# The one-hot rows of a gate matrix: two scalars in one VectorE instruction, the other rows on POOL

## The chip, the cores and the metric

The kernel runs on one NeuronCore of a Trainium2 chip. Its engines work side by side and meet only at semaphores: TensorE (PE) multiplies matrices into PSUM, VectorE (DVE) and ScalarE (ACT) work on PSUM and SBUF, GpSimd (POOL) on SBUF, and SyncE (SP) issues DMAs. The metric is the device time of one execution in microseconds (us); lower is better.

## The reference, cut to what matters

Four layers run one after another on 256 tokens of width 1024: two of a first kind and two of a second kind. The change lies in the last part of each second-kind layer, a feed-forward with 16384 small experts. A token picks 8 x 16 experts, and each expert number is a pair of key numbers below 128:

```python
cand_i = top_i[:, :, 0, :, None] * N_KEYS + top_i[:, :, 1, None, :]
best_s, best_pos = lax.top_k(cand_s..., PEER_TOPK)
experts = take_along_axis(cand_i..., best_pos)
gate = jax.nn.softmax(best_s, axis=-1)
act = jax.nn.gelu(einsum('td,thkd->thk', t, expert_down[experts]))
return einsum('thk,thkd->td', (gate * act), expert_up[experts])
```

## The kernel before, in words

`peer(l)` doesn't gather experts. It computes all 16384 activations densely, multiplies them by a gate matrix that is zero for experts not picked, and multiplies the product with all of `expert_up`. Everything is fp32, and a weight tile is split into a rounded part `hi` and a rest `lo`, so that three matmul passes give the product.

The weights come in units of 128x1024: 16 of the query projection (`PQ`), 128 of `expert_down`, 128 of `expert_up`. Each unit goes through a ring of three buffers (`RING`): SP loads it into `raw` (L1774), ACT writes `hi` (`head`, L1891), the rest `lo` is written by POOL for the first `BY_POOL` = 86 units (L1795) and by DVE for later ones (`rest`, L2057), then PE uses it: `down(n)` issues 24 matmuls (L1810), `up(x)` 12 (L1843). SP loads a buffer again once `lo` of the unit before in it is written.

Between units 72 (`PQ + FIRST`) and 83 lies **the gate stage**. The three picks of each token (first key number, second key number, softmax gate) have been turned by PE so that a token is a column of `i1T`, `i2T` and `gT`, with its 128 picks along the partitions. For each of 64 groups (`GROUPS`) of 4 tokens (`GROUP`):

- DVE (`one_hots`, L2043) compares `iota` with 4 columns of `i1T` at once into `hot1`, and with 4 columns of `i2T` into `hot2`, two instructions of 512 elements per partition. There are three buffers of each (`HOTS`); from the fourth group on it waits until PE has used the third last.
- ACT (`gated`, L1922) multiplies the four rows of `hot1` by the token's gate, four instructions of 128 elements in place, and signals `gated`.
- PE (`gates`, L1830) multiplies `hot2` with `hot1` for each token, a 128x128 gate matrix each, into one of four PSUM banks. The trace shows 8 matmul records for a group.
- DVE (`into_a`, L2051) multiplies the first 56 columns of the bank into the activations `A`, two groups behind `one_hots`; ACT (`to_a`, L1928) copies the other 72 columns to `A`.

After 11 of the 64 groups (`STAGED`, by `staged_after`: after group 5, 11, 17, 23, 29 and so on to 63) PE does one `down` unit; ACT then takes its result (L1905) and does `head` for the unit three ahead, after which POOL writes that unit's `lo`. ACT's order in the loop is: `gated(g + 1)`, `to_a(g)`, and where a unit was due after group g - 1, its result and a `head`. When the stage is over DVE multiplies the 11 staged units in one instruction (L2097), and PE does the other 61 `down` units. The stage occurs once in each of the two second-kind layers.

## Time and profile before

| | us |
|---|---|
| time, median of 3 executions | 3636.59 (3634.34 to 3645.01) |
| the profiled execution's own time | 3646.36 |
| its span, first to last instruction | 3643.6 |
| PE busy in it | 3080.6 (85%) |
| DVE busy | 2466.6 (68%) |
| ACT busy | 1530.2 (42%) |
| POOL busy | 1040.1 (29%) |

Durations of the profile belong to an execution of 3646.36 us, 2.8 us of them outside the span. The two layers with a gate stage fill the second half of the span: their gate stages lie at about 1856 to 2015 and 2950 to 3111 us from its start. An instruction's duration in the trace overlaps a little with the next one's on DVE, ACT and PE, so how much an instruction of a row adds is read from one start to the next; both are called here by name, duration and pitch. A wait for another engine's semaphore stands as idle time before an instruction; a wait for an SBUF port stands inside its duration.

### The profile page before, as it was taken

The numbers are of one execution on the slowest core, as the hardware profiler recorded it, in microseconds if no ns is written. First come the engines' busy times: TensorE is split into PE (matmuls) and PEld (weight loads), VectorE is DVE, ScalarE is ACT, GpSimd is POOL, SyncE is SP. The second block draws the span as 40 slices with busy tenths as digits, with TensorE's granted clock in tenths as the row PEclk, the third lists the DMA queues.
The fourth block names the chain that finished last, engine by engine and source line by source line (L and its number), as shares of the span: only waits on it lengthen the run. The fifth ranks groups of instructions, "written<-read, shape, count | busy, mean of one in ns | idle before, by whom it ended". The sixth has DMA issues, their size and how long they took to land. (4 is left out here: it accounts for less than half of the span.)

```text
span 3643.6 us, 48268 instructions
## 1 busy us (share of the span) xinstructions
PE 3080.6 (85%) x18164; PEld 2737.8 (75%) x18164; DVE 2466.6 (68%) x3633; ACT 1530.2 (42%) x2506; POOL 1040.1 (29%) x559
## 2 busy tenths in 40 slices
PE   6765899867758997859987999998869987999998
PEld 5654677666646765749977998886759986998887
DVE  5998756569987664537958655665547958655665
ACT  2221443222215432324467444553324467444554
POOL 3355520543555114008941000000007941000000
PEclk9887899988879999769988999999779998999999
DMA  5444444454434444505631566665505631566665
GB/s 211 147 146 145 179 160 152 155 214 150 159 134 185 153 145 179 179 22 183 186 104 36 170 190 185 205 193 156 198 12 181 186 110 41 158 190 186 204 195 162
DMA packets 128230, 568.86 MB, mean 156 GB/s; under 512 B 14155, under 2 KB 24172, under 8 KB 96364
## 3 DMA queue, kind: packets, MB, share of 16 engines
q1 hardware_dynamic: 117916, 505.43, 42.7%
q0 software_dynamic: 9216, 56.63, 4.3%
q8 instruction: 148, 2.42, 0.3%
q10 hardware_dynamic: 864, 3.67, 0.2%
q14 instruction: 86, 0.70, 0.1%
HBM read 551.52 MB, written 15.20 MB: 156 GB/s over the span
## 5 line engine op out<-in xcount | busy, mean ns | idle before, releaser
L1810 PE MATMUL e_ps<-k_hhi,e_hi 128*128 128x256 f32 x2304 | 651.6, 283 | 30.2 <-POOL e_lo L1795 30.2
L1810 PE MATMUL e_ps<-k_hlo,e_hi 128*128 128x256 f32 x2304 | 645.9, 280 | 0.0
L1810 PE MATMUL e_ps<-k_hhi,e_lo 128*128 128x256 f32 x2304 | 644.3, 280 | 0.0
L2057 DVE TENSOR_TENSOR e_lo<-e_raw,e_hi 128x1024 fp32r<-128x1024 f32 x372 | 455.9, 1226 | 193.9 <-ACT e_hi L1891 193.9
L1891 ACT ACTIVATE e_hi<-e_raw 128x1024 fp32r<-128x1024 f32 x544 | 571.0, 1050 | 26.7 <-DMA e_raw<-down 26.1
L1795 POOL TENSOR_TENSOR e_lo<-e_raw,e_hi 128x1024 fp32r<-128x1024 f32 x172 | 444.6, 2599 | 344.1 <-ACT e_hi L1891 343.5
L721 DVE TENSOR_TENSOR f_wlo<-f_raw,f_whi 128x2048 fp32r<-128x2048 f32 x156 | 390.5, 2519 | 191.8 <-ACT f_whi L539 191.8
L539 ACT ACTIVATE f_whi<-f_raw 128x2048 fp32r<-128x2048 f32 x156 | 296.2, 1911 | 505.7 <-DMA f_raw<-ws 391.1
L1810 PEld LDWEIGHTS e_ps<-k_hhi,e_hi 128*128 128x128 f32 x2304 | 436.3, 189 | 31.6 <-POOL e_lo L1795 31.2
L1810 PEld LDWEIGHTS e_ps<-k_hlo,e_hi 128*128 128x128 f32 x2304 | 436.5, 189 | 0.0
L1810 PEld LDWEIGHTS e_ps<-k_hhi,e_lo 128*128 128x128 f32 x2304 | 435.9, 189 | 0.0
L1843 PE MATMUL e_ps<-e_hi,e_ghi 128*128 128x512 f32 x1024 | 315.4, 389 | 1.2 <-DVE e_glo L2066 1.2
L1843 PE MATMUL e_ps<-e_hi,e_glo 128*128 128x512 f32 x1024 | 315.3, 389 | 0.0
L1843 PE MATMUL e_ps<-e_lo,e_ghi 128*128 128x512 f32 x1024 | 315.2, 389 | 0.0
L412 PE MATMUL f_psA<-f_whi,k_hhi 128*128 128x512 f32 x672 | 276.9, 412 | 44.0 <-DVE f_wlo L721 38.4
L774 DVE SCALAR_TENSOR_TENSOR f_cy<-f_vpad,f_par,f_cy 128x256 f32<-128x256 f32 x480 | 313.9, 725 | 0.0
L389 PE MATMUL f_psA<-k_hhi,f_whi 128*128 128x256 f32 x640 | 200.0, 312 | 117.2 <-DVE f_wlo L721 103.8
L690 POOL TENSOR_TENSOR f_x<-f_x,k_cact 128x2048 f32<-128x2048 f32 x48 | 216.6, 4513 | 273.4 <-DMA f_x<-ada 273.4
L692 POOL TENSOR_TENSOR f_x<-f_x 128x1024 f32<-128x1024 f32 x144 | 268.7, 1866 | 11.3
L412 PE MATMUL f_psA<-f_wlo,k_hhi 128*128 128x512 f32 x672 | 271.9, 405 | 0.0
L412 PE MATMUL f_psA<-f_whi,k_hlo 128*128 128x512 f32 x672 | 271.2, 404 | 0.0
L1940 ACT ACTIVATE e_ghi<-e_a 128x256 fp32r<-128x256 f32 x256 | 107.0, 418 | 344.8 <-PE e_ps L1843 344.8
(335 smaller groups left out, 5749.1 us busy)
## 6 DMA issues: line engine op xcount, KB each, us to landing
f_raw<-ws SPq DMA_DIRECT2D x156, 1024.0 KB, 5.0
e_raw<-down SPq DMA_DIRECT2D x288, 512.0 KB, 3.7
e_raw<-up SPq DMA_DIRECT2D x256, 512.0 KB, 3.7
f_x<-ada POOLq DMA_DIRECT2D x48, 1024.0 KB, 5.3
s_raw<-ws SPq DMA_DIRECT2D x24, 1024.0 KB, 5.1
mod_parts<-f_x POOLq DMA_DIRECT2D x48, 128.0 KB, 2.0
s_parts<-mod_parts SPq DMA_DIRECT2D x8, 768.0 KB, 8.7
f_x<-out SPq DMA_DIRECT2D x4, 1024.0 KB, 5.1
```

The costliest lines, as they stand in the source:

```text
L389: last = nc.tensor.matmul(psA[:, n % 4, f * T:(f + 1) * T], w[:, c:c + P], x[:, kt, :], start=kt == 0 and i == 0, stop=kt == KT - 1 and i ...
L412: last = nc.tensor.matmul(psA[:, (n + t) % 4, :], x[:, kt, ts_], w[:, k * CH:(k + 1) * CH], start=v == 0 and k == 0 and i == 0, stop=v == ...
L539: nc.scalar.activation(w_hi[:, u % NW, :], raw[:, u % NRAW, :], ACT.Copy).then_inc(S["hi_ready"], 1)
L690: own.link(nc.gpsimd.tensor_tensor(a3, a3, by_c, ALU.mult))
L692: own.link(nc.gpsimd.tensor_tensor(ada[:, 0:half], ada[:, 0:half], ada[:, half:2 * half], ALU.add))
L721: V.tensor_tensor(w_lo[:, u % NW, :], raw[:, u % NRAW, :], w_hi[:, u % NW, :].bitcast(F32), ALU.subtract).then_inc(S["lo_ready"], 1)
L774: ins = V.scalar_tensor_tensor(cy[:, ft, :], v, w, cy[:, ft, :], ALU.mult, ALU.add)
L1795: nc.gpsimd.tensor_tensor(lo[:, i % RING, :], raw[:, i % RING, :], hi[:, i % RING, :].bitcast(F32), ALU.subtract).then_inc(S["lo_pool"], 1)
L1810: last = nc.tensor.matmul(psD(n), w, h, start=kt == 0 and i == 0, stop=kt == KT - 1 and i == 2)
L1843: last = nc.tensor.matmul(psY(t, c), g[:, b, tok], w[:, r, c * CH:(c + 1) * CH], start=x == 0 and i == 0, stop=x == NE - 1 and i == 2)
L1891: nc.scalar.activation(hi[:, i % RING, :], raw[:, i % RING, :], ACT.Copy).then_inc(S["hi_ready"], 1)
L2057: V.tensor_tensor(lo[:, i % RING, :], raw[:, i % RING, :], hi[:, i % RING, :].bitcast(F32), ALU.subtract).then_inc(S["lo_dve"], 1)
```

## The change

`hot1` is now written by DVE row by row with the gate in it: one `tensor_scalar` of 128 elements for a token, with two per-partition scalars, `(iota == i1T[:, t]) * gT[:, t]`, four for a group. `hot2` is written by POOL, one `tensor_scalar` of 128 elements for a token with one per-partition scalar, `iota == i2T[:, t]`. ACT's `gated` and its semaphore are gone: PE waits for `hot1_ready` and `hot2_ready`. POOL stops writing `lo` at unit 75 (`BY_POOL` = 75), then does its 256 rows; units 75 to 85 get their `lo` from DVE, ten inside the loop of groups, four groups behind the unit that they follow, and one behind the loop.

```diff
-BY_POOL = PQ + FIRST + STAGED + RING
+BY_POOL = PQ + FIRST + RING
...
+                pool.wait_ge(S["in_const"], 32)
+                pool.wait_ge(S["picks_copied"], 2)
+                for g in range(GROUPS):
+                    if g >= HOTS:
+                        pool.wait_ge(S["w_mm"], g - HOTS + 1)
+                    for k in range(GROUP):
+                        t = g * GROUP + k
+                        ins = nc.gpsimd.tensor_scalar(hot2[:, g % HOTS, k, :], iota[:, :], i2T[:, t:t + 1], None, ALU.is_equal)
+                    ins.then_inc(S["hot2_ready"], 1)
...
-                    pe.wait_ge(S["gated"], g + 1)
+                    pe.wait_ge(S["hot1_ready"], g + 1)
                     pe.wait_ge(S["hot2_ready"], g + 1)
...
-                def gated(g):
-
-                    act.wait_ge(S["hot1_ready"], g + 1)
-                    for k in range(GROUP):
-                        row = hot1[:, g % HOTS, k, :]
-                        ins = nc.scalar.activation(row, row, ACT.Copy, scale=gT[:, g * GROUP + k:g * GROUP + k + 1])
-                    ins.then_inc(S["gated"], 1)
...
-                gated(0)
                 for g in range(GROUPS):
-                    if g + 1 < GROUPS:
-                        gated(g + 1)
                     to_a(g)
...
-                    tokens = slice(g * GROUP, (g + 1) * GROUP)
-                    for hot, picks, ready in ((hot1, i1T, "hot1_ready"), (hot2, i2T, "hot2_ready")):
-                        V.tensor_tensor(hot[:, g % HOTS, :, :], iota[:, :].rearrange("p (a n) -> p a n", a=1).to_broadcast([P, GROUP, NE]),
-                                        picks[:, tokens].rearrange("p (a n) -> p a n", n=1).to_broadcast([P, GROUP, NE]),
-                                        ALU.is_equal).then_inc(S[ready], 1)
+                    for k in range(GROUP):
+                        t = g * GROUP + k
+                        ins = V.tensor_scalar(hot1[:, g % HOTS, k, :], iota[:, :], i1T[:, t:t + 1], gT[:, t:t + 1], ALU.is_equal, ALU.mult)
+                    ins.then_inc(S["hot1_ready"], 1)
...
                 for g in range(GROUPS):
-                    one_hots(g)
+                    gated(g)
                     if g >= 2:
                         into_a(g - 2)
+                    n = staged_after(g - 4) if g >= 4 else None
+                    if n is not None:
+                        rest(n + RING)
                 into_a(GROUPS - 2)
                 into_a(GROUPS - 1)
+                for g in range(GROUPS - 4, GROUPS):
+                    n = staged_after(g)
+                    if n is not None:
+                        rest(n + RING)
```

DVE's row in the gate stage before, from the group whose `into_a` is the seventh (the `e_hot` names are `hot1` and `hot2`):

```order
L2051 TENSOR_TENSOR e_a<-e_ps,e_a 128x56x4
L2043 TENSOR_TENSOR e_hot_6867<-e_iota,e_i1T 128x512
L2043 TENSOR_TENSOR e_hot_6868<-e_iota,e_i2T 128x512
L2051 TENSOR_TENSOR e_a<-e_ps,e_a 128x56x4
L2043 TENSOR_TENSOR e_hot_6867<-e_iota,e_i1T 128x512
L2043 TENSOR_TENSOR e_hot_6868<-e_iota,e_i2T 128x512
```

And DVE's row there in the change:

```order
L2049 TENSOR_TENSOR e_a<-e_ps,e_a 128x56x4
L2042 TENSOR_SCALAR e_hot_6867<-e_iota,e_i1T,e_gT 128x128 x4
L2049 TENSOR_TENSOR e_a<-e_ps,e_a 128x56x4
L2055 TENSOR_TENSOR e_lo<-e_raw,e_hi 128x1024
L2042 TENSOR_SCALAR e_hot_6867<-e_iota,e_i1T,e_gT 128x128 x4
L2049 TENSOR_TENSOR e_a<-e_ps,e_a 128x56x4
```

Two wide compares became four short instructions, and the rest of a weight unit stands between two groups. ACT's row around the first staged unit before:

```order
L1922 ACTIVATE e_hot_6867<-e_hot_6867,e_gT 128x128 x4
L1928 ACTIVATE e_a<-e_ps 128x72x4
L1905 ACTIVATE e_b<-e_ps 128x256
L1891 ACTIVATE e_hi<-e_raw 128x1024
L1922 ACTIVATE e_hot_6867<-e_hot_6867,e_gT 128x128 x4
L1928 ACTIVATE e_a<-e_ps 128x72x4
```

And in the change:

```order
L1930 ACTIVATE e_a<-e_ps 128x72x4 x7
L1915 ACTIVATE e_b<-e_ps 128x256
L1901 ACTIVATE e_hi<-e_raw 128x1024
L1930 ACTIVATE e_a<-e_ps 128x72x4 x6
L1915 ACTIVATE e_b<-e_ps 128x256
L1901 ACTIVATE e_hi<-e_raw 128x1024
```

The gate copies that stood behind each `head` are gone from ACT. POOL's whole row for `peer` in the change against before:

```order
 L996 ISA
 L1791 UNCONDITIONAL_BRANCH
-L1795 TENSOR_TENSOR e_lo<-e_raw,e_hi 128x1024 x86
+L1795 TENSOR_TENSOR e_lo<-e_raw,e_hi 128x1024 x75
+L1805 TENSOR_SCALAR e_hot_6868<-e_iota,e_i2T 128x128 x256
 L1761 UNCONDITIONAL_BRANCH
```

Eleven long instructions left POOL, and 256 short ones came behind the other 75.

## Rows read from the trace of the kernel before

**Rows 1.** Stretches: length, each engine's busy time, granted TensorE clock, DMA share, GB/s.

```profile
1856.00:2015.00 159.00, 118.11 (x810) 111.10 (x809) 127.05 (x196) 114.00 (x345) 31.38 (x13) 0.87 0.15 44
...
2950.00:3111.00 161.00, 119.41 (x830) 112.14 (x829) 124.24 (x195) 114.76 (x347) 34.64 (x14) 0.88 0.16 48
```

**Rows 2.** Groups of 1860 to 2012: busy us, mean ns; idle before, its releasers.

```profile
L1830 PE MATMUL e_ps<-e_hot,e_hot 128*128 128x128 f32 x512 | 84.7, 328 | 40.9 <-ACT e_hot L1922 36.5 <-DVE e_hot L2043 4.3
...
L2043 DVE TENSOR_TENSOR e_hot<-e_iota,e_i2T 128x512 f32<-128x512 f32 x64 | 67.5, 1055 | 0.0
L2043 DVE TENSOR_TENSOR e_hot<-e_iota,e_i1T 128x512 f32<-128x512 f32 x63 | 42.9, 681 | 0.0
L2051 DVE TENSOR_TENSOR e_a<-e_ps,e_a 128x224 f32<-128x224 f32 x64 | 24.8, 388 | 29.0 <-PE e_ps L1830 27.5
...
L1922 ACT ACTIVATE e_hot<-e_hot,e_gT 128x128 f32<-128x128 f32 x252 | 79.8, 392 | 2.1 <-DVE e_hot L2043 2.1
...
L1891 ACT ACTIVATE e_hi<-e_raw 128x1024 fp32r<-128x1024 f32 x11 | 11.6, 1058 | 0.0
...
L1795 POOL TENSOR_TENSOR e_lo<-e_raw,e_hi 128x1024 fp32r<-128x1024 f32 x10 | 25.7, 2573 | 119.5 <-ACT e_hi L1891 119.5
```

**Rows 3.** Timeline behind one staged unit: start us, length us, engine, line.

```profile
1943.18 1.95 PE L1830 MATMUL e_ps<-e_hot,e_hot 128*128 128x128 f32 x16
1947.54 1.26 PE L1830 MATMUL e_ps<-e_hot,e_hot 128*128 128x128 f32 x8 [2.41 <-ACT e_hot L1922]
...
1945.78 0.38 DVE L2051 TENSOR_TENSOR e_a<-e_ps,e_a 128x224 f32<-128x224 f32 x1
1946.09 0.68 DVE L2043 TENSOR_TENSOR e_hot<-e_iota,e_i1T 128x512 f32<-128x512 f32 x1
1946.68 2.84 DVE L2043 TENSOR_TENSOR e_hot<-e_iota,e_i2T 128x512 f32<-128x512 f32 x1
...
1946.22 1.27 ACT L1922 ACTIVATE e_hot<-e_hot,e_gT 128x128 f32<-128x128 f32 x4
...
1946.41 2.58 POOL L1795 TENSOR_TENSOR e_lo<-e_raw,e_hi 128x1024 fp32r<-128x1024 f32 x1 [9.74 <-ACT e_hi L1891]
```

**Rows 4.** The stretch that follows it, columns as in rows 1.

```profile
1949.40:1954.80 5.40, 4.99 (x23) 4.70 (x23) 4.42 (x10) 3.92 (x13) 0.00 (x0) 0.50 0.33 99
```

**Rows 5.** Timeline: the first gate matmul, and the instruction behind the stage.

```profile
1860.50 0.77 PE L1830 MATMUL e_ps<-e_hot,e_hot 128*128 128x128 f32 x2 [4.34 <-DVE e_hot L2043]
...
2012.04 3.09 DVE L2097 TENSOR_TENSOR e_a<-e_a,e_b 128x2816 f32<-128x2816 f32 x1 [2.90 <-ACT e_b L1905]
```

**Rows 6.** DVE's tensor_scalar, two lines (ns min/median/max) and a timeline row.

```profile
L1655 DVE TENSOR_SCALAR s_ys<-s_ys,s_stat x4: 346/348/348, 1587.2 to 2685.5; 128x256 f32<-128x256 f32 x4
L1655 DVE TENSOR_SCALAR s_ya<-s_ya,s_stat x4: 479/480/482, 1587.7 to 2686.1; 128x512 f32<-128x512 f32 x4
...
369.75 2.67 DVE L896 TENSOR_SCALAR f_cy<-f_cy,f_par 128x256 f32<-128x256 f32 x8
```

**Rows 7.** POOL's nearest instructions, grouped or by line, in ns.

```profile
L1449 POOL TENSOR_SCALAR s_stat<-s_stat 128x8 f32<-128x8 f32 x6 | 1.2, 200 | 134.5 <-DVE s_stat L1539 91.8 <-DVE s_stat L1591 42.5
L1453 POOL MEMSET s_ones<- 128x128 f32 x2 | 0.4, 202 | 0.0
...
L692 POOL TENSOR_TENSOR f_x<-f_x x144: 724/1335/4539, 44.4 to 1434.1; 128x1024 f32<-128x1024 f32 x48, 128x512 f32<-128x512 f32 x48, 128x256 f32<-128x256 f32 x48
```

**Rows 8.** Timeline of DVE and POOL instructions that overlap, in two places.

```profile
70.17 1.36 POOL L692 TENSOR_TENSOR f_x<-f_x 128x512 f32<-128x512 f32 x1
71.61 0.81 POOL L692 TENSOR_TENSOR f_x<-f_x 128x256 f32<-128x256 f32 x1
71.74 0.95 DVE L774 SCALAR_TENSOR_TENSOR f_cy<-f_vpad,f_par,f_cy 128x256 f32<-128x256 f32 x1
...
1704.72 2.41 POOL L1795 TENSOR_TENSOR e_lo<-e_raw,e_hi 128x1024 fp32r<-128x1024 f32 x1 [0.18 <-ACT e_hi L1891]
1706.44 0.72 DVE L2025 TENSOR_SCALAR e_bx<-e_bp 128x32 uint32<-128x32 uint32 x1
```

More of the change, by code:

```diff
@@ L1744, in peer @@
         names = """in_const in_keys raw0 raw1 raw2 in_x out_x hi_ready lo_pool lo_dve unit_done psd_read score_mm sc_copied
-            dve_step t_sub t_exp iv_ready picks_mm picks_copied hot1_ready hot2_ready gated w_mm w_read_dve w_read_act
+            dve_step t_sub t_exp iv_ready picks_mm picks_copied hot1_ready hot2_ready w_mm w_read_dve w_read_act
             staged_mult weighted g_hi_ready g_lo_ready gate_mm gate_ready prod_done x_done""".split()
@@ L2035, in key_numbers, with gated @@
                     own.step(V.tensor_reduce(iv[:, 0:2, :, h * 16:(h + 1) * 16].rearrange("p k t s -> p (k t) s"), hots[:, :, :, :], AX.X, ALU.add))
-                def one_hots(g):
+                def gated(g):
                     if g >= HOTS:
                         dve.wait_ge(S["w_mm"], g - HOTS + 1)
-                    tokens = slice(g * GROUP, (g + 1) * GROUP)
-                    for hot, picks, ready in ((hot1, i1T, "hot1_ready"), (hot2, i2T, "hot2_ready")):
-                        V.tensor_tensor(hot[:, g % HOTS, :, :], iota[:, :].rearrange("p (a n) -> p a n", a=1).to_broadcast([P, GROUP, NE]),
-                                        picks[:, tokens].rearrange("p (a n) -> p a n", n=1).to_broadcast([P, GROUP, NE]),
-                                        ALU.is_equal).then_inc(S[ready], 1)
+                    for k in range(GROUP):
+                        t = g * GROUP + k
+                        ins = V.tensor_scalar(hot1[:, g % HOTS, k, :], iota[:, :], i1T[:, t:t + 1], gT[:, t:t + 1], ALU.is_equal, ALU.mult)
+                    ins.then_inc(S["hot1_ready"], 1)
                 def into_a(g):
```

## The prediction, made before the change was run

> **What bounds the kernel now.** I read the stretches first. Over the gate stages PE is busy for only 118 of 159 us and 119 of 161 us, at a mean granted clock of 0.87 and 0.88 of full [rows 1]. DVE (127 us) and ACT (114 us) are busier than they look necessary for 64 groups, and POOL has 31 us. So these two stretches, 320 us of 3644, are where an exchange between DVE, ACT and POOL can move the end.
>
> Next I read the groups of one stage by shape. Each of the 64 groups costs DVE two compares of 512 elements and one `into_a`. Their pitches stand in the timeline: `into_a` starts at 1945.78, the next compare at 1946.09, the next at 1946.68 [rows 3], so 0.31 and 0.60 us. A group is 2 x 0.60 + 0.31 = 1.51 us, 64 of them 97 us. The second compare has a mean of 1055 ns where the first has 681 [rows 2]: 64 x 0.374 = 24 us more. The timeline shows what that is: the compare at 1946.68 lasts 2.84 us because POOL's `lo` instruction runs from 1946.41 to 1948.99, and it ends 0.53 us behind it [rows 3]. Eleven such collisions of 2.17 us make the 24. DVE then waits 29 us for PE [rows 2]. 97 + 24 + 29 = 150, and the stage from the first gate matmul to the multiply behind it lasts 2012.04 - 1860.50 = 151.5 us [rows 5]. The account closes.
>
> Why does DVE wait for PE if PE is idle for 41 us? PE's idle time is put down to ACT's gate copies, 36.5 us [rows 2]. Behind each staged unit ACT does a result, a `head` of 1.06 us [rows 2] and only then the copies at 1946.22 for the next group; PE, whose two ready groups ended at 1945.13, stands for 2.41 us [rows 3]. A few microseconds later the granted clock is 0.50, that is 1.2 GHz instead of 2.4, for 5.4 us [rows 4]. There PE is busy and slow. So the stage is bound by a loop DVE, ACT, PE with three faults in each of 11 rounds: the copies behind a `head`, the collision with POOL, and the half clock behind the idle time.
>
> **What the change removes.** ACT loses 256 copies a stage, 80 us of duration [rows 2], and PE no longer waits for ACT's order. DVE loses both compares, 1.20 us a group, and the collisions with the long POOL instruction, 24 us a stage. POOL loses 11 instructions of 2.57 us.
>
> **What it adds on DVE.** A `tensor_scalar` of 256 elements takes 348 ns and one of 512 takes 480 [rows 6], so 128 elements less save 66 ns. With two scalars, eight of 256 elements last 2.67 us [rows 6]; the last one's duration being 0.41 (0.35 and about 0.06 for the second scalar), the pitch is (2.67 - 0.41) / 7 = 0.32 us. For 128 elements I get 0.32 - 0.066 = 0.256 us, four of them 1.02, and with `into_a` 1.33 us a group. Against 1.51 that is little: cut in four, the work of the same 512 elements costs more than one wide compare did, and the gain on DVE is only that `hot2` went elsewhere. The moved `lo` adds 11 x 1.15 us = 12.7 us; its price is not in the gate stage of before, and I take POOL's 2.57 halved less a short overlap, since both engines do the same instruction and the compare of 512 elements on DVE (0.60) scales to 1.14 for 1024 elements. Nothing is past it in DVE's queue but the next group, and POOL and PE have up to three groups of rows in hand. DMA isn't touched: SP's load of a later unit waits for this `lo`, some 2 us later than before, but three units of about 9 us lie between.
>
> **What it adds on POOL.** Nothing in the trace is this instruction: one input of 128 elements, one per-partition scalar. The nearest below is the `tensor_scalar` of 8 elements, 200 ns, and a memset of 128 elements, 202 ns. The nearest above is a two-input instruction: 128x256 takes at least 724 ns [rows 7] and 128x1024 takes 2573 [rows 2], 2.41 ns an element, so 128 elements would take 724 - 308 = 416 ns. One input at half that rate makes 200 + 144 = 344 ns, which I take; the ends are 200 and 416. A gain below nothing is excluded, since it is work that POOL did not have.
>
> **How the two disturb each other.** DVE's `tensor_scalar` in fp32 from SBUF to SBUF collides with POOL: at 1706.44 one of 32 elements lasts 0.72 us, until POOL's instruction ends at 1707.13 [rows 8]. The price of turns can be read from the first layers: POOL's instruction of 512 elements ends at 71.53, its next of 256 ends at 72.42, and the DVE instruction in between ends its own turn 0.27 us behind that [rows 8]. From end to end 0.89 us pass, of which 0.27 are DVE's turn, so POOL's turn is 0.62 where alone it takes 0.724: 0.10 us of its fixed part runs beside DVE's turn. DVE's turn is its streaming time alone. For the change: POOL's turn 0.344 - 0.10 = 0.24 us (bounds 0.10 and 0.32), DVE's turn 0.066 + 0.02 = 0.09. If both always took turns, four pairs last 1.32 us, and a DVE group 1.32 + 0.31 = 1.63; if POOL's turns fall wholly beside `into_a` and DVE's fixed parts, 1.33 remain. I take 1.50, in the middle.
>
> The Trainium skill ("SBUF — State Buffer", Who interferes with whom) says that a VectorE instruction in a two-port mode and a GpSimd instruction exclude each other for the whole instruction, whoever starts first. The row at 1706.44 agrees; the row at 71.61 limits it to less than the duration. What the rule would make of the time by its words is the last rival. The same notes ("VectorE: DVE Perf Modes", The TRN2 errata) advise tiles of at least 512 elements because each instruction pays a fixed cost, which speaks against the cut in four; by the rows 1.02 against 0.60 us it is true here, and the sum above holds it already.
>
> **The sum.** 64 x 1.50 = 96 us; the moved `lo` 12.7; a wait at each staged unit, because PE is away for 2.9 us while DVE may run only three groups ahead, and `lo` waits for a `head`: 11 x 0.7 = 7.7 us (an estimate: three groups of 1.5 us cover the unit, but not the `head` of 1.06 behind it); the first gate matmul comes 0.6 us later, since POOL makes its four rows after its last `lo`; the last unit and its result 3.2 us. Together 120 us. PE needs less: 8 records of about 0.12 us, 0.95 us, for 64 groups and 11 x 2.9, 93 us at full clock. Against 151.5 the stage is 31 us shorter, and both stages 62. Behind the stage DVE does one `lo` more ahead of its multiply, 1.15 us in a stretch where PE has three units ready: nothing is lost. The profiled execution would go from 3646.4 to 3584, and the median from 3636.6 to **3574 us**. With a POOL turn of 0.10 and 1.33 us a group it is 109 us, 85 saved, 3552; with a turn of 0.32 and no overlap (4 x 0.41 + 0.31 = 1.95) it is 149 us, 5 saved, 3632.
>
> **The rivals.**
> - *The turns eat the gain.* POOL's instruction is nearer to the two-input row, pairs cost 0.41 us or a little more, the waits move from ACT to the port: 3625 to 3640, say 3632. For it: a software loop per element on POOL, shown by 2.41 ns an element. Chance 0.12.
> - *POOL becomes the bound, slower than before.* A per-partition scalar and a compare may cost POOL more than any row shows. The stage is worse than before when a group costs over (151.5 - 24) / 64 = 1.99 us, that is when POOL's turn passes 0.41. At a turn of 0.60 a group is 4 x 0.69 = 2.76 us, the stage 201 us, the kernel 99 us slower: 3735. Against it: the 8-element row has fixed costs of only 200 ns. Chance 0.10.
> - *The clock stays low.* If PE runs the gate matmuls at 1.2 GHz throughout, a group takes PE 1.75 us, the stage 64 x 1.75 + 32 = 144 and with the start 147: 9 us saved, 3628. For it: rows 4. Against it: the 2.4 us of idle time ahead of it goes. Chance 0.07.
> - *DVE doesn't get its fast form* with a compare and two scalars: 0.32 us each, but then no turns with POOL. 4 x 0.32 + 0.31 = 1.6, stage 126, 3586. Chance 0.07.
> - *The port is held for whole durations*, as the page says: 0.34 for POOL and 0.34 for DVE, 2.72 us a group, stage 198, two stages 93 us longer, 3730. The row at 71.61 speaks against it. Chance 0.04.
>
> **How the numbers follow.** My forecast, a stage of 109 to 135 us, has 0.60. A measurement of this kernel can tell about 0.3%, 11 us. Faster by more than that: 0.60, the slow DVE form 0.07, part of the first and third rival 0.08, in all 0.75. Within: 0.11. Slower: 0.14. The range from 3545 to 3640 leaves out the two slow rivals and the best corner of the forecast.
>
> **What would show it.** Right: between the first gate matmul and the multiply behind the stage 120 us in place of 151.5; DVE's new instruction at a mean of 0.34 to 0.45 us with POOL's at about 0.35 to 0.45; PE's idle time in the stage below 20 us and put down to DVE or POOL; granted clock above 0.95. Wrong: POOL's instruction above 0.5 us, a POOL without idle time and PE waiting for it; a clock of 0.50 over most of the stage; or DVE waiting for ACT's `head` ahead of the moved `lo` for more than 1 us a time.

## The result and the profile after

The changed kernel takes 3661.53 us, median of 6 executions (3657.72 to 3667.01), where the kernel before took 3639.14 on the same chip, median of 6 (3631.52 to 3645.01). The ratio is 1.0072, with a 95% interval from 1.0052 to 1.0092: slower by 0.7%, 22 us. The prediction said 3574, with a range up to 3640. It had the wrong sign, and the result lies 21.5 us outside the range.

The first and the last row of a gate stage, in the timeline of the changed kernel (start, length, engine, line, in brackets the idle time before), answer to [rows 5]:

```profile
1860.51 0.77 PE L1840 MATMUL e_ps<-e_hot,e_hot 128*128 128x128 f32 x2 [5.87 <-POOL e_hot L1805]
...
2023.38 3.08 DVE L2102 TENSOR_TENSOR e_a<-e_a,e_b 128x2816 f32<-128x2816 f32 x1
```

The stage lasts 2023.38 - 1860.51 = 162.9 us where it was 151.5. The second layer's stage lasts 162.7 where it was 151.1. The two differences, 11.4 and 11.6 us, are 23 us, as much as the medians differ by (22). The two profiled executions differ by less, 18 us in their spans; the other 5 lie outside the gate stages and are not traced here. Every stage length below is read between these two rows, in the first and in the second layer.

The stretch 1875 to 1970 lies inside the stage in every kernel of this study. Here it is, for the kernel before and then for the changed one, in the columns of [rows 1] (length; busy us of PE, PEld, DVE, ACT, POOL; granted clock; DMA share; GB/s):

```profile
1875.00:1970.00 95.00, 72.15 (x475) 67.92 (x474) 78.13 (x122) 70.56 (x216) 18.02 (x7) 0.84 0.13 40
```

```profile
1875.00:1970.00 95.00, 65.48 (x477) 61.42 (x475) 66.41 (x202) 23.47 (x53) 95.00 (x154) 0.93 0.12 39
```

ACT fell from 71 to 23 us, DVE from 78 to 66, and the granted clock rose from 0.84 to 0.93: ACT's gate copies and most of the slow clock are gone. But POOL is busy for 95.00 of 95 us. The groups of one stage (1860 to 2012) show who waits, in the columns of [rows 2]:

```profile
L1840 PE MATMUL e_ps<-e_hot,e_hot 128*128 128x128 f32 x496 | 75.7, 306 | 50.7 <-issue 25.4 <-DVE e_hot L2042 17.6 <-POOL e_hot L1805 7.6
...
L2042 DVE TENSOR_SCALAR e_hot<-e_iota,e_i1T,e_gT 128x128 f32<-128x128 f32 x247 | 75.3, 373 | 0.0
L2049 DVE TENSOR_TENSOR e_a<-e_ps,e_a 128x224 f32<-128x224 f32 x61 | 23.5, 385 | 44.8 <-PE e_ps L1840 44.8
L2055 DVE TENSOR_TENSOR e_lo<-e_raw,e_hi 128x1024 fp32r<-128x1024 f32 x10 | 13.2, 1323 | 2.8 <-ACT e_hi L1901 2.8
...
L1805 POOL TENSOR_SCALAR e_hot<-e_iota,e_i2T 128x128 f32<-128x128 f32 x248 | 152.7, 638 | 0.0
```

PE no longer waits for ACT at all, yet it is idle for 51 us in place of 41, and DVE waits for PE for 45 us in place of 29. The releasers named here don't name the bound: PE and DVE wait for each other (17.6 and 44.8 us), and 25.4 us stand under "issue", with no releaser in the profile. The engine to look for is the one with no idle time, and that is POOL; the runs below test it. The timeline has all its rows of the stage in one line, and the line's own entry has the durations (ns, min/median/max):

```profile
1858.01 157.39 POOL L1805 TENSOR_SCALAR e_hot<-e_iota,e_i2T 128x128 f32<-128x128 f32 x256
```

```profile
L1805 POOL TENSOR_SCALAR e_hot<-e_iota,e_i2T x512: 596/602/1681, 1858.0 to 3122.9; 128x128 f32<-128x128 f32 x171
```

256 instructions of a median 0.602 us follow each other for 157.4 us, 0.615 each. The stage is that queue: it starts when four rows are there and ends 8.0 us behind the last one (1858.01 + 157.39 = 2015.40).

The mean of the rows is 638 ns and their median 602, so a few rows are much longer than the rest. They are the rows that meet one of DVE's moved `lo`. One such pair, DVE's and POOL's:

```profile
1910.64 1.30 DVE L2055 TENSOR_TENSOR e_lo<-e_raw,e_hi 128x1024 fp32r<-128x1024 f32 x1 [0.30 <-ACT e_hi L1901]
```

```profile
1911.08 1.33 POOL L1805 TENSOR_SCALAR e_hot<-e_iota,e_i2T 128x128 f32<-128x128 f32 x1
```

The row takes 1.33 us in place of 0.60: it ends at 1912.41, 0.47 us behind `lo`. The first stage has ten such rows, one for each `lo` between its groups, 7.3 us more than the usual 0.60 in all; the ten of the second stage cost 8.8 us. On a queue without idle time all of this is time of the stage. So the moved `lo` costs twice, once on DVE and once on POOL.

### The profile page after: what moved, and what is told of

It is laid out like the page before. It is cut to its first block and busy times, and to the rows that moved or that the text cites. A ratio compares the mean times of both kernels' runs of the same rounds, so it can differ in the third digit from the quotient of the medians.

```text
span 3661.7 us, 48526 instructions
## 1 busy us (share of the span) xinstructions
PE 3077.7 (84%) x18164; PEld 2735.5 (75%) x18164; DVE 2435.0 (66%) x3911; ACT 1383.6 (38%) x1994; POOL 1290.5 (35%) x1049
## 5 line engine op out<-in xcount | busy, mean ns | idle before, releaser
L2055 DVE TENSOR_TENSOR e_lo<-e_raw,e_hi 128x1024 fp32r<-128x1024 f32 x394 | 484.2, 1229 | 206.2 <-ACT e_hi L1901 205.8
L1795 POOL TENSOR_TENSOR e_lo<-e_raw,e_hi 128x1024 fp32r<-128x1024 f32 x150 | 382.3, 2564 | 91.8 <-ACT e_hi L1901 90.4
L1805 POOL TENSOR_SCALAR e_hot<-e_iota,e_i2T 128x128 f32<-128x128 f32 x512 | 316.0, 640 | 0.0
```

Of the source, the lines that this page charges most:

```text
L1795: nc.gpsimd.tensor_tensor(lo[:, i % RING, :], raw[:, i % RING, :], hi[:, i % RING, :].bitcast(F32), ALU.subtract).then_inc(S["lo_pool"], 1)
L1805: ins = nc.gpsimd.tensor_scalar(hot2[:, g % HOTS, k, :], iota[:, :], i2T[:, t:t + 1], None, ALU.is_equal)
L2055: V.tensor_tensor(lo[:, i % RING, :], raw[:, i % RING, :], hi[:, i % RING, :].bitcast(F32), ALU.subtract).then_inc(S["lo_dve"], 1)
```

## The experiments

### The price of POOL's instruction

`probe_forms` adds a few instructions of each form at the end of POOL's program, when PE is through with the gate matrices, and nothing else (one execution, 3652.18 us):

```diff
+                for i in range(6):
+                    ins = G.tensor_scalar(row(i), iota[:, :], i2T[:, i:i + 1], None, ALU.is_equal)
...
+                    ins = G.tensor_scalar(row(i), iota[:, :], 5.0, None, ALU.is_equal)
...
+                    ins = G.tensor_scalar(row(i), iota[:, :], i2T[:, i:i + 1], None, ALU.mult)
...
+                    ins = G.tensor_scalar(row(i)[:, 0:8], iota[:, 0:8], i2T[:, i:i + 1], None, ALU.is_equal)
...
+                for i in range(3):
+                    ins = G.tensor_scalar(four(i), wide, i2T[:, i:i + 1], None, ALU.is_equal)
...
+                    ins = G.tensor_tensor(row(i), iota[:, :], i2T[:, i:i + 1].to_broadcast([P, NE]), ALU.subtract)
```

> The changed kernel, and behind POOL's 256 rows, where POOL has nothing else to do, seven short series of POOL instructions into a buffer that nobody reads any more: (1) the row instruction of the change, 128 elements, compare with a per-partition scalar; (2) the same with an immediate; (3) multiply in place of compare; (4) 8 elements; (5) 512 elements; (6) a two-input subtract of 128 elements; (7) a two-input subtract of 512. Theory A (the price is POOL's own fixed cost of a per-partition scalar): (1) stays at 0.60 us away from DVE's instructions, (3) and (4) lie within 0.15 us of it, (2) falls to 0.30 to 0.35, (5) costs 0.3 to 0.5 more than (1). Theory B (the price is per element, a slow loop for the compare): (4) is near 0.25, (5) near 1.8 us. Theory C (the 0.60 is mostly waiting for the port behind DVE): (1) falls below 0.45 here. The series add about 20 us of POOL beside the rest of the layer; the time stays within 0.3% of the changed kernel's 3661.

Its lines, each with ns min/median/max (DVE was at work at times, so the minimum is the undisturbed value), and the timeline's row for the first six:

```profile
L1815 POOL TENSOR_SCALAR e_hot<-e_iota,e_i2T x12: 601/602/603, 2004.4 to 3116.4; 128x128 f32<-128x128 f32 x12
L1819 POOL TENSOR_SCALAR e_hot<-e_iota x12: 526/1490/3035, 2008.0 to 3124.5; 128x128 f32<-128x128 f32 x12
L1823 POOL TENSOR_SCALAR e_hot<-e_iota,e_i2T x12: 593/601/1672, 2017.0 to 3131.0; 128x128 f32<-128x128 f32 x12
L1827 POOL TENSOR_SCALAR e_hot<-e_iota,e_i2T x12: 301/310/1257, 2022.6 to 3134.1; 128x8 f32<-128x8 f32 x12
L1831 POOL TENSOR_SCALAR e_hot<-e_iota,e_i2T x6: 1561/1654/2527, 2025.6 to 3137.9; 128x512 f32<-128x512 f32 x6
L1835 POOL TENSOR_TENSOR e_hot<-e_iota,e_i2T x12: 395/489/1382, 2031.2 to 3143.4; 128x128 f32<-128x128 f32 x12
L1839 POOL TENSOR_TENSOR e_hot<-e_iota,e_i2T x6: 1041/1222/2018, 2035.4 to 3147.1; 128x512 f32<-128x512 f32 x6
```

```profile
2004.40 3.49 POOL L1815 TENSOR_SCALAR e_hot<-e_iota,e_i2T 128x128 f32<-128x128 f32 x6 [1.41 <-PE e_ps L1875]
```

And a row of the changed kernel's timeline, eleven of its POOL rows beside DVE's gated rows:

```profile
1899.96 6.48 POOL L1805 TENSOR_SCALAR e_hot<-e_iota,e_i2T 128x128 f32<-128x128 f32 x11
```

From 8 to 128 elements the duration grows by 300 ns, 2.50 ns an element; from 128 to 512 by 960 ns, 2.50 again. So the instruction costs 0.28 us and 2.50 ns an element with **one** input, no less than the two-input `lo` (2.41 ns in the prediction). A multiply costs what the compare costs; the pointer to the scalar (the scalar is read from SBUF, not given in the instruction) adds 601 - 526 = 75 ns; a `tensor_tensor` whose second input is broadcast costs less, (1041 - 395) / 384 = 1.68 ns an element. Alone the pitch is (3.49 - 0.60) / 5 = 0.578 us; beside DVE's gated rows it is (6.48 - 0.60) / 10 = 0.588. The instruction is dear by its elements, and DVE's gated rows have next to no part in its price. The theory of a large fixed cost falls with the 8-element row.

`rows8` asks whether the rest of the prediction's sum holds once POOL's rows are cheap. The buffers are cleared once, and each row has 8 elements, so the kernel leaves out most of the gate matrix:

```diff
-                        ins = nc.gpsimd.tensor_scalar(hot2[:, g % HOTS, k, :], iota[:, :], i2T[:, t:t + 1], None, ALU.is_equal)
+                        ins = nc.gpsimd.tensor_scalar(hot2[:, g % HOTS, k, 0:8], iota[:, 0:8], i2T[:, t:t + 1], None, ALU.is_equal)
```

> The changed kernel with POOL's 256 row instructions cut to 8 of the 128 elements each (the rest of hot2 stays at zero from one memset, so most of the gate matrix is missing); all other instructions, waits and their numbers are the change's. From the forms run a row then costs POOL 0.29 us start to start, near the price that the prediction had assumed. Theory A (the price of the POOL row was the only wrong term of the prediction's sum): the stage falls from 163 to 112 to 126 us, the kernel to 3565 to 3590. Theory D (the rest of the sum was wrong as well: DVE's turns, waits at the staged units, PE's clock): the stage stays above 135 us, 3610 or more.

Measured: 3568.24 against 3627.89, ratio 0.9834 (0.981 to 0.9857), stages of 119.9 and 118.9 us. The stretch 1875 to 1970 and POOL's group in it:

```profile
1875.00:1970.00 95.00, 78.51 (x635) 75.46 (x635) 79.59 (x262) 31.22 (x70) 71.86 (x199) 0.98 0.17 50
```

```profile
L1807 POOL TENSOR_SCALAR e_hot<-e_iota,e_i2T 128x8 f32<-128x8 f32 x199 | 72.1, 412 | 20.6 <-PE e_ps L1842 20.6
```

POOL now waits for PE for 20.6 us and is no longer the bound. The prediction's stage of 120 us and its 62 us saved are there (-60), as soon as POOL's row is not 0.60. DVE's groups of the whole first stage (1855 to 1975) tell how the 120 us come about:

```profile
L2044 DVE TENSOR_SCALAR e_hot<-e_iota,e_i1T,e_gT 128x128 f32<-128x128 f32 x246 | 69.4, 351 | 0.0
L2051 DVE TENSOR_TENSOR e_a<-e_ps,e_a 128x224 f32<-128x224 f32 x64 | 24.8, 389 | 15.6 <-PE e_ps L1842 15.6
L2057 DVE TENSOR_TENSOR e_lo<-e_raw,e_hi 128x1024 fp32r<-128x1024 f32 x11 | 13.5, 1225 | 6.9 <-ACT e_hi L1903 6.9
```

A gated row (one of the four instructions of `hot1`) has a mean of 351 ns, nearly the 346 without POOL (`dve_all`, below), so a group costs DVE about 1.35 us. 64 x 1.35 = 86 us, 12.5 of `lo` and 22.5 of waits (15.6 + 6.9) are the 120, to within 1 us.

`rows64` is the same edit with 64 elements, and leaves out half of the gate matrix. It puts POOL at a price between the two, to find where its queue takes over:

```diff
+                        ins = nc.gpsimd.tensor_scalar(hot2[:, g % HOTS, k, 0:64], iota[:, 0:64], i2T[:, t:t + 1], None, ALU.is_equal)
```

> As the run with 8 elements a row, with 64 (half of hot2's columns stay zero). From the forms run a row costs POOL 0.286 + 56 x 0.00247 = 0.42 us start to start, 1.70 a group. Theory A (POOL's queue binds wherever four rows cost more than DVE's 1.5 to 1.6 us a group): the stage is 64 x 1.70 + 11 x 0.7 + 6 = 123 to 132 us, the ratio to the kernel before 0.985 to 0.990, between 8 elements (0.983, 119 us) and 128 (1.007, 163 us), and nearer to 8. If the turns at the port were what costs, the time would lie halfway, at a stage of about 141 us and a ratio of 0.995.

Measured: 3605.41 against 3639.80, 0.9905 (0.9881 to 0.9929), stages of 132.6 and 133.2 us, both just above what was expected:

```profile
1875.00:1970.00 95.00, 74.68 (x575) 71.11 (x574) 75.05 (x243) 28.16 (x63) 92.09 (x190) 0.95 0.15 45
```

190 rows in 92.1 us are 0.485 each. The probe's 8-element row (0.301), less the 0.024 by which rows overlap (0.602 - 0.578), and 56 x 2.5 ns give 0.42. So some 0.06 us a row is what DVE adds here. By the durations of single rows about half of it is the eight rows of this stretch that start beside a `lo` (each about 1.0 us longer), and the other half comes from gated rows. With 8, 64 and 128 elements the stage lasts 119, 133 and 163 us. The last step is POOL's queue, 256 x (0.615 - 0.485) = 33 us against 30 measured; at 8 elements another bound holds.

### Which half of the change costs, and which pays

`pool_part` keeps only POOL's half and the moved `lo`. `hot1` is again one wide compare of DVE and four gate copies of ACT, `hot2` is POOL's:

```diff
-                    for k in range(GROUP):
-                        t = g * GROUP + k
-                        ins = V.tensor_scalar(hot1[:, g % HOTS, k, :], iota[:, :], i1T[:, t:t + 1], gT[:, t:t + 1], ALU.is_equal, ALU.mult)
-                    ins.then_inc(S["hot1_ready"], 1)
+                    tokens = slice(g * GROUP, (g + 1) * GROUP)
+                    V.tensor_tensor(hot1[:, g % HOTS, :, :], iota[:, :].rearrange("p (a n) -> p a n", a=1).to_broadcast([P, GROUP, NE]),
+                                    i1T[:, tokens].rearrange("p (a n) -> p a n", n=1).to_broadcast([P, GROUP, NE]),
+                                    ALU.is_equal).then_inc(S["hot1_ready"], 1)
```

> Only the POOL half of the change: hot2 by POOL's rows and lo of units 75 to 85 by DVE, but hot1 by one wide compare on DVE and gated by ACT's four copies, as before. Theory A: POOL's queue is the bound here too; each group 4 x 0.58 = 2.32 us and more, because the wide compare of 0.60 us reads through the port that POOL needs, 0 to 0.5 us a group: 3660 to 3715, never below the changed kernel by over 0.3%. Theory D (the loss came from the short DVE instructions): back to before or better, 3640 or less.

Measured: 3705.47 against 3638.17, 1.0182 (1.0163 to 1.0201), stages of 182.9 and 184.6 us. POOL's group in 1875 to 1970:

```profile
L1805 POOL TENSOR_SCALAR e_hot<-e_iota,e_i2T 128x128 f32<-128x128 f32 x136 | 95.6, 724 | 0.4 <-PE e_ps L1840 0.4
```

The same instruction has a mean of 724 ns where it had 638. Away from DVE's `lo` a row that overlaps a wide compare, which reads two inputs from SBUF, has a mean of 0.76 us, the others 0.60. Rows that start beside a `lo` with a wide compare behind it last 1.9 us; they make about half of the excess in this stretch. The stretch shows POOL again without idle time, DVE busy for less than half, and PE at a granted clock of 0.78:

```profile
1875.00:1970.00 95.00, 67.12 (x401) 62.43 (x402) 41.47 (x73) 59.98 (x184) 94.59 (x136) 0.78 0.11 34
```

`dve_all` keeps DVE's half and takes POOL out of the stage: `hot1` by four gated rows, `hot2` by the old wide compare on DVE, no gate copies, `lo` by DVE as in the change:

```diff
+                    V.tensor_tensor(hot2[:, g % HOTS, :, :], iota[:, :].rearrange("p (a n) -> p a n", a=1).to_broadcast([P, GROUP, NE]),
+                                    i2T[:, tokens].rearrange("p (a n) -> p a n", n=1).to_broadcast([P, GROUP, NE]),
+                                    ALU.is_equal).then_inc(S["hot2_ready"], 1)
```

> The change without POOL in the stage: DVE writes hot1 as in the change (four short instructions with two scalars) and hot2 as before (one compare of 512 elements); ACT has no gate copies and DVE writes lo of units 75 to 85. It tells what the other half of the change is worth. Theory A: the ACT half gains on its own; DVE's group is 4 x 0.256 + 0.60 + 0.31 = 1.93 us, the stage 64 x 1.93 + 12.7 + 7.7 + 3.2 = 147 us, 4 us less than before each: 3625 to 3635. If ACT's copies were the true bound of before, 3600 or less; if they were no bound at all and DVE's work alone counts, 1.93 against 1.51 us a group shows, and the time is above 3660.

Measured: 3621.08, 0.9943 (0.9924 to 0.9962), stages of 143.5 and 144.9 us, a little better than expected. DVE's groups from 1860 to 2010, and the stretch 1875 to 1970:

```profile
L2033 DVE TENSOR_SCALAR e_hot<-e_iota,e_i1T,e_gT 128x128 f32<-128x128 f32 x256 | 72.8, 346 | 0.0
L2036 DVE TENSOR_TENSOR e_hot<-e_iota,e_i2T 128x512 f32<-128x512 f32 x64 | 43.6, 682 | 0.0
L2044 DVE TENSOR_TENSOR e_a<-e_ps,e_a 128x224 f32<-128x224 f32 x64 | 24.4, 382 | 5.1 <-PE e_ps L1831 5.1
```

```profile
1875.00:1970.00 95.00, 75.57 (x522) 71.92 (x522) 91.95 (x268) 26.18 (x57) 0.00 (x0) 0.86 0.13 40
```

DVE is the bound, 92 of 95 us. Gated rows and `lo` on DVE together gain 17 us with no help from POOL (the two are taken apart under "What the collisions were worth"). Moving `hot2` to POOL on top of them makes the stage 19 us longer, 143.5 to 162.9: that is the sign of the result.

`split3` and `split2` divide the rows of `hot2`, three or two to POOL and the rest to DVE as one-scalar rows:

```diff
-                    for k in range(GROUP):
+                    for k in range(3):
...
+                    for k in range(3, GROUP):
+                        t = g * GROUP + k
+                        ins = V.tensor_scalar(hot2[:, g % HOTS, k, :], iota[:, :], i2T[:, t:t + 1], None, ALU.is_equal)
```

> The change, but POOL writes three of a group's four hot2 rows and DVE the fourth. Theory A (a POOL row costs 0.58 us start to start, and POOL's queue is the bound of the stage): POOL's group falls from 2.32 to 1.74 us, the stage from 163 to about 126 to 132 us, each stage 20 to 25 us shorter than before the change, 3590 to 3600. Theory C (port turns with DVE are the bound): one row moved from POOL to DVE changes nothing in the sum of turns; 3645 to 3665. Theory D (the stage is held by PE's clock or its dependencies, and POOL only looks busy): 3650 to 3662.

Measured: 3610.24 against 3638.17, 0.9921 (0.9903 to 0.9939), stages of 137.1 and 138.4 us; expected were 126 to 132. The miss is in what POOL's rows cost now. Of 1860 to 2010:

```profile
L1805 POOL TENSOR_SCALAR e_hot<-e_iota,e_i2T 128x128 f32<-128x128 f32 x192 | 129.1, 692 | 3.2 <-PE e_ps L1840 3.2
```

192 rows fill 129.1 us, 0.672 each: 0.09 more than alone, 18 us in all. Ten rows that last over 1 us beside DVE's `lo` make 8.8 of the 18; the rest, some 0.05 us a row, comes with the gated and the one-scalar rows of DVE. POOL waits for only 3.2 us and is still the bound, though with a quarter of its work gone. With two rows to DVE (the same edit with 2 in place of 3):

> As the version with three rows on POOL and one on DVE, but two and two. POOL 2 x 0.60 = 1.2 us a group plus turns; DVE 4 x 0.27 + 2 x 0.21 + 0.31 = 1.8 and 0.2 for lo, so DVE is the bound: stage 64 x 2.0 + 6 = 134 us, about that of three and one (137): 3598 to 3615. If turns at the port were what binds three and one, fewer POOL rows would free DVE and give under 3590.

Measured: 3612.87 against 3627.89, 0.9948 (0.9928 to 0.9967), stages of 138.2 and 139.1 us. Its stretch 1875 to 1970 shows that the bound has changed sides, DVE being busy for 91 and POOL for 65 of 95 us:

```profile
1875.00:1970.00 95.00, 75.97 (x559) 72.06 (x559) 90.53 (x324) 28.69 (x62) 65.33 (x91) 0.91 0.13 40
```

Three rows and two rows give stages of equal length from two sides: between these two engines alone 137 us is about what there is. (Two and three rows in turn were not tried.)

### What the collisions were worth

`dve_all` has POOL's long `lo` instructions moved to DVE. `dve_lo_pool` is `dve_all` with them left on POOL:

```diff
-BY_POOL = PQ + FIRST + RING
+BY_POOL = PQ + FIRST + STAGED + RING
```

> hot1 and hot2 by DVE (short rows with the gate, and one wide compare), no gate copies on ACT, but POOL keeps writing lo of units 75 to 85 as before the change. Against the version where DVE writes them (3621, stage 144 us) DVE saves 11 x 1.15 = 12.7 us a stage and gets 11 collisions: with the two-port form it waits 2.1 to 2.4 us for POOL's long instruction each, 23 to 26 us. Expected: stage 154 us, 3636 to 3650. If short instructions pass beside POOL's long one, 3600 or less.

Measured: 3650.50 against 3627.89, 1.005 (1.003 to 1.0069), stages of 157.1 and 156.8 us, 12 to 14 us longer than with `lo` on DVE. One collision in its timeline, POOL's row and three of DVE's:

```profile
1900.53 1.11 DVE L2033 TENSOR_SCALAR e_hot<-e_iota,e_i1T,e_gT 128x128 f32<-128x128 f32 x4
...
1902.44 3.10 DVE L2033 TENSOR_SCALAR e_hot<-e_iota,e_i1T,e_gT 128x128 f32<-128x128 f32 x4
1905.47 0.68 DVE L2036 TENSOR_TENSOR e_hot<-e_iota,e_i2T 128x512 f32<-128x512 f32 x1
...
1902.35 2.35 POOL L1795 TENSOR_TENSOR e_lo<-e_raw,e_hi 128x1024 fp32r<-128x1024 f32 x1 [11.81 <-ACT e_hi L1892]
```

Four gated rows that take 1.11 us take 3.10 beside `lo`: 1.99 us lost, much as the wide compare lost 2.17 in [rows 3]. From 1860 to 2010 DVE's rows have a mean of 428 in place of 346 ns, 256 x 0.082 = 21 us:

```profile
L2033 DVE TENSOR_SCALAR e_hot<-e_iota,e_i1T,e_gT 128x128 f32<-128x128 f32 x244 | 87.8, 428 | 0.0
```

This is what moving `lo` buys, for the 13.4 us that its eleven instructions are busy on DVE in `dve_all`. And it is what makes `dve_all` a gain: with gated rows alone and `lo` left on POOL the kernel is 0.5% slower than before. In the changed kernel the moved `lo` also stops POOL, for 7.3 us a stage. No run there leaves `lo` on POOL; by its durations that would put 11 x 2.57 = 28 us on the queue that is the bound, so moving it is still the better of the two. Whether the moved `lo` would have paid in the kernel before, with nothing else changed, was not tried.

### Rows for the idle engine

In the changed kernel ACT is idle for three quarters of the stage. `act_share` gives it two of the four rows of `hot2`, as relu(1 - |i2T - iota|), which is one where they are equal and zero elsewhere. POOL makes the other two:

```diff
-                    for k in range(GROUP):
+                    for k in range(2):
...
+                def distances(g):
...
+                        ins = nc.scalar.activation(hot2[:, g % HOTS, 2 + k, :], iota[:, :], ACT.Abs, bias=i2T[:, t:t + 1], scale=-1.0)
+                    ins.then_inc(S["dist_ready"], 1)
+
+                def hot_rows(g):
+
+                    act.wait_ge(S["dist_ready"], g + 1)
+                    nc.scalar.activation(hot2[:, g % HOTS, 2:4, :], hot2[:, g % HOTS, 2:4, :], ACT.Relu, bias=1.0, scale=-1.0).then_inc(S["hot2a_ready"], 1)
...
                 for g in range(GROUPS):
+                    if g + 2 < GROUPS:
+                        distances(g + 2)
                     to_a(g)
+                    if g + 2 < GROUPS:
+                        hot_rows(g + 2)
```

> The change with hot2's rows shared: POOL writes two of four rows, ScalarE the other two, as relu(1 - abs(i2T - iota)), two instructions of 128 elements and one of 256, one group ahead of its copy to A and never behind a head of the same round. DVE has only hot1's four rows and into_a. Per group then POOL 2 x 0.58 = 1.2 us, ACT about 0.6 + 0.3 + 0.3 and a share of 0.25 for the staged units, 1.45, DVE 1.33 and 0.2 for lo. Theory A: no engine has more than 1.6 us a group, the stage is 112 to 128 us: 3565 to 3595, faster than the kernel before and than the version with three rows on POOL (3610). If ACT's order still makes PE wait behind each staged unit, as before the change: 3610 to 3630.

Measured: 3606.81 against 3627.89, 0.9937 (0.9914 to 0.9961), stages of 144.1 and 142.5 us, far from the expected 112 to 128. The stretch, and the waits (who waits <- releaser: us, times, longest) of 1875 to 1970, point to a reason:

```profile
1875.00:1970.00 95.00, 73.77 (x521) 70.22 (x519) 67.50 (x218) 62.68 (x183) 58.56 (x86) 0.89 0.13 40
```

```profile
ACT e_a L1945 <- DVE e_a L2074: 32.7, 27, 2.7
...
PE e_ps L1841 <- ACT e_hot L1940: 15.7, 13, 1.3
```

`to_a(g)` waits for DVE's `into_a`, and it stood in ACT's queue ahead of the second step for two groups later. `act_share2` puts both steps ahead of `to_a`:

```diff
                     if g + 2 < GROUPS:
                         distances(g + 2)
+                        hot_rows(g + 2)
                     to_a(g)
-                    if g + 2 < GROUPS:
-                        hot_rows(g + 2)
```

> As the version that shares hot2's rows between POOL and ScalarE, with one line moved: ScalarE writes both steps of its rows for group g + 2 ahead of its copy for group g, where before the second step stood behind that copy, which waits for DVE. In the profile of the first form PE waited 20 us in 115 for exactly that second step. Theory A (the order of waits on ScalarE held it): these waits go, the stage falls from 143 to 118 to 130 us, and the ratio to the kernel before to 0.980 to 0.988. Theory E (POOL's two rows, each up to 0.70 us beside DVE's instructions, or PE's clock hold it): 140 us or more, ratio 0.992 or more.

Measured: 3588.25 against 3639.80, 0.9856 (0.9829 to 0.9883), stages of 126.7 and 124.7 us. It is faster than both kernels, by 1.4% than the one before. Its stretch 1875 to 1970, and three waits there:

```profile
1875.00:1970.00 95.00, 76.55 (x584) 72.20 (x584) 77.92 (x256) 76.12 (x213) 65.27 (x99) 0.95 0.17 50
```

```profile
POOL e_hot L1805 <- PE e_ps L1841: 28.9, 27, 2.6
PE e_ps L1841 <- ACT e_hot L1940: 17.5, 15, 1.6
ACT e_a L1945 <- DVE e_a L2073: 17.2, 17, 2.4
```

No engine is full, and POOL has time to spare. The new order shortens the stage by 17 us, as theory A forecast, but not in the way that it gave: the wait that was to go is still there. PE stands for ACT's second step for 17.5 us in a stretch that has 49 groups, where it stood 15.7 us in one that has 44 (392 and 352 matmul records, 8 a group), 0.36 us a group both times. What did fall is ACT's wait for DVE, from 32.7 to 17.2 us, and the granted clock rose from 0.89 to 0.95. Which of these carries the gain, and what would clear the rest, is open.

`split3_again` is `split3` on the chip of `act_share2`, so that the two can be set against one another:

> The same kernel as split3 (three of four hot2 rows on POOL, one on DVE), for a comparison on one chip with the version that shares the rows with ScalarE. Ratio to the kernel before again 0.990 to 0.994; the sharing version should be below it by 0.4 to 1.2% if theory A of its own run holds.

Measured: 3608.01, 0.9912 (0.989 to 0.9933), stages of 134.9 and 135.9 us. This agrees with `split3`; the version with ACT is ahead by 20 us on one chip.

## Why the prediction was wrong, point by point

- **The step that failed is the price of POOL's row**, under "What it adds on POOL": "One input at half that rate makes 200 + 144 = 344 ns, which I take; the ends are 200 and 416." It is 602 ns, above the upper end. Two things were too low. The rate is 2.50 ns with one input, where I halved 2.41; and the 8-element row [rows 7] has no pointer scalar, which costs 75 ns. The upper end was no bound: I took a two-input instruction to be dearer than a one-input one, which no row showed. The same rows without the halving give 0.20 + 128 x 0.00241 = 0.51 us, a queue of 256 x 0.51 = 131 us that is already longer than my 120 us stage; with the 5.5 us at its ends (below) the stage is 136 us and still a gain. The pointer's 256 x 0.075 = 19 us take that gain away.
- **A second term was put at nothing: what DVE's moved `lo` does to POOL.** The prediction priced `lo` on DVE alone (12.7 us). Alone, 256 rows at their pitch of 0.578 us are 148 us, with the ends 153.5, two more than the 151.5 of before: no loss that this measurement could tell. The rest of the 162.9 is 7.3 us of rows stopped by `lo` and some 2 us from gated rows. So of the 43 us by which the stage misses the 120, 34 are POOL's price; of the 11 us by which it is worse than before, 7 are `lo`. The 7.3 us are counted from the durations in the trace; no run takes `lo` off both engines.
- The Trainium skill ("GPSIMD Engine Reference", 3.1 Elementwise — side-by-side cycle accounting) has the same idea: it puts the 2.6 cycles an element of a two-input instruction down to two inputs taking turns at one read port, and bodies of one or two operations at 1.03 cycles. The probe differs for this instruction: 2.50 ns an element with one input, and 1.68 with two when one of them is broadcast. The measurement decides: the number of inputs alone is not what sets this rate.
- **The rival "POOL becomes the bound" is what happened, with a wrong threshold and price.** It took the group's price up to 1.99 us to be harmless, and at a turn of 0.60 it gave 3735. Both came from adding DVE's turns of 0.09 to each of POOL's, and 24 us of `lo`, units and start to the sum. Of these only `lo` touches POOL's queue, by its stops of 7.3 us. The stage is 256 x 0.615 = 157.4 us and 5.5 at the ends (8.0 behind the last row, less the 2.5 by which the first rows are ahead of the first matmul), so it loses from (151.5 - 5.5) / 256 = 0.57 us a row on, stops included, and at 0.615 it loses 11 us.
- **"How the two disturb each other" holds for neither engine as a price of turns.** I took 1.50 us for a group where 1.33 is undisturbed, 0.04 us for each gated row; they have a mean of 373 ns beside a POOL without idle time and 346 without POOL, 0.03, but only 351 in `rows8`. POOL's rows were to lose 0.09 us a turn. In the changed kernel they lose 0.01 beside gated rows (0.588 against 0.578), in `rows8` the median row is 0.384 us where it is 0.301 alone, and beside a `lo` a row loses 0.73 us at once. One price for a turn doesn't describe this. One reading was also wrong: the instruction at 1706.44 [rows 8] that is called fp32 works on uint32.
- **Right by its total, in part by luck**: with POOL's row cheap (`rows8`) a stage lasts 120 us (119.9 and 118.9) and 60 us are saved, where 120 and 62 were forecast. But two terms miss by some 10 us each and cancel: DVE's 64 groups take 86 us and not 96 (1.35 us a group and not 1.50), and its waits take 22.5 us where the staged units, the later start and the last unit were given 11.5 (7.7 + 0.6 + 3.2). Right in themselves are the end of ACT's faults and the clock that follows (0.84 before, 0.98), the gated row's pitch, given as 0.256, which is (1.11 - 0.346) / 3 = 0.255 in the undisturbed row of `dve_lo_pool`, and `lo` on DVE at about the given 12.7 us (13.4 and 13.5 busy in `dve_all` and `rows8`, by durations, which overlap a little). `lo` waits for `head` 0.3 us a time in the changed kernel, where 1 us was the sign of an error.
- **Too low**: the first gate matmul waits 5.87 us where it was 4.34 [rows 5], 1.5 us later and not 0.6; four rows of POOL at 0.60 in place of 0.344 are 1.0 of it.
- **The signs to look for** were the right ones. "POOL's instruction above 0.5 us, a POOL without idle time and PE waiting for it" stood there as the mark of a wrong prediction, and is what the profile shows.
- **The other rivals**: the slow form of DVE is out (0.255 us), the clock that stays low is out (0.93), and the port held for whole durations is out for gated rows against POOL's rows (last section), though it is close to what happens beside `lo`.

## What to carry to other kernels

Before `tensor_scalar` rows in fp32 go to POOL, multiply elements by 2.5 ns, add 0.28 us, multiply by the count, and hold this queue alone against the stage; here 256 x 0.60 = 154 us stand against a whole stage of 151.5. Then add what the other engine's long instructions do to this queue: here 0.73 us for each `lo` on DVE. A bound from "the nearest row above" needs a row that shows the assumed order; where none does, the price is open upward, and a rival must carry more than one chance in ten. Where an engine's queue is the bound, divide its rows over all the engines with time left (`act_share2`, the fastest of the kernels here that compute the whole result). On an engine that runs in order, putting what others wait for ahead of what waits itself gained 17 us a stage, though not by the wait that was its reason.

## What the runs showed of the hardware

- POOL's `tensor_scalar` in fp32 costs 0.28 us, 75 ns of it for the pointer scalar, and 2.50 ns an element, compare and multiply alike. `tensor_tensor` with one broadcast input costs 1.68 ns an element. Why the form with fewer inputs is the slower one is not settled.
- The contention on DVE's and POOL's port depends on the pair. DVE's gated rows are stopped for the rest of POOL's two-input `lo` (1.11 to 3.10 us for four), but lose 0.03 us each beside POOL's one-input rows. The Trainium skill ("SBUF — State Buffer", Who interferes with whom) has a DVE instruction in a two-port mode and a GpSimd instruction exclude each other, one of the two blocked for the whole instruction of the other. The row of `lo` agrees; beside a POOL that has no gap in 157 us, a gated row would then wait for half of a POOL row, some 0.3 us (an estimate from 0.60 us), and it does not. That POOL's one-input form holds the port for only a part of its time, or takes it differently, is a guess that no run here tests.
- The other way round, DVE's instructions with two SBUF inputs stop POOL's rows. In the changed kernel a row that meets DVE's `lo` of 1.30 us lasts 1.33 us in place of 0.60, and up to 1.68; in `pool_part` rows beside a wide compare have a mean of 0.76 us.
- Short POOL rows are slowed by DVE's gated rows more than long ones: 8 elements 0.384 us (median of `rows8`) against 0.301 alone, 128 elements 0.588 against 0.578 from start to start. Why is not settled.
- A `tensor_scalar` of 128 elements with two pointer scalars has a pitch of 0.255 us on DVE and does a compare and a multiply in it: four gated rows (1.02 us) replace a wide compare (0.60 us) and four ACT copies (1.27 us).
